# Query, index-query and z projections with 512 moving columns per matmul, in slabs of half the contraction

## What is computed

```
h = rmsnorm(x, attn_norm)
q, k, v, iq, ik, iw, z, xbc, dt, gate_a, gate_b = split(h @ w_in)     # widths 1024, 256, 256, 512, 64, 8, 2048, ...
q, k, iq, ik: head norms and partial rope
y_attn = sparse attention(q, k, v, iq, ik, iw)
y_ssd  = state-space scan(conv(xbc), dt)
y = y_ssd * silu(z)
y_ssd = y * rsqrt(mean(y^2) over each of 4 groups of 512) * ssd_norm
merged = sigmoid(gate_a) * (y_attn @ w_attn_branch) + sigmoid(gate_b) * (y_ssd @ w_ssd_branch)
```

## Time and profile before

| | |
|---|---|
| median of 3 runs | 1435.93 us (1435.58 to 1440.99) |
| the profiled execution | 1435.79 us |
| its span, first to last instruction | 1434.0 us |
| mean granted clock of TensorE | 0.969 |
| PE busy | 1341.9 us (94%) |
| PEld, DVE, ACT, POOL busy | 1223.3, 933.8, 755.3, 197.5 us |
| q to iq, on PE | 675.7 to 721.8 us |
| z, on PE | 971.5 to 1019.5 us |

### The profile page before, as it was taken

How to read it: one execution, slowest core, us unless ns; L and a number is a source line. 1 busy time by engine, 2 the same in 40 slices (tenths; PEclk the granted TensorE clock), 3 DMA queues, 4 the chain that set the end, 5 groups by cost and what they waited for, 6 DMA issues and landing times.

```text
span 1434.0 us, 22961 instructions
## 1 busy us (share of the span) xinstructions
PE 1341.9 (94%) x9038; PEld 1223.3 (85%) x9038; DVE 933.8 (65%) x1331; ACT 755.3 (53%) x1108; POOL 197.5 (14%) x163
## 2 busy tenths in 40 slices
PE   5999999979898999998989897989999999999998
PEld 5999989979698999988979787889999877787776
DVE  4655554474575555565379674584664799999996
ACT  4334345545634333355445676333653577778774
POOL 0211120021001111120020331230000000202020
PEclk9999999999999999999989899998999899999999
DMA  7666554533153665644634333324555399999991
GB/s 246 211 189 188 179 162 151 176 118 118 37 162 116 205 188 181 190 148 131 187 90 141 96 118 119 89 59 123 172 176 181 122 365 367 367 367 338 369 342 64
DMA packets 222165, 263.43 MB, mean 184 GB/s; under 512 B 14018, under 2 KB 204799, under 8 KB 221951
## 3 DMA queue, kind: packets, MB, share of 16 engines
q1 hardware_dynamic: 219520, 260.39, 56.8%
q10 hardware_dynamic: 2558, 1.86, 0.4%
HBM read 261.17 MB, written 1.05 MB: 183 GB/s over the span
## 4 chain that ended last, share of the span: by engine, by line
PE 75%; DVE 14%; ACT 6%; issue 2%; POOL 1%; DMA 1%; ACTq 0%; DVEq 0%; POOLq 0%
PE bank L526 23%; PE bank L528 22%; PE bank L527 22%; DVE sb_wlo L483 3%; DVE sb_wlo L470 3%; PE bank L621 1%; DVE sb_XC L1880 1%; PE bank L2502 1%; ACT sb_whi L464 1%; ACT sb_aw L1546 1%; DMA sb_pos<-in_positions 1%; DVE sb_st L1120 1%; PE bank L2565 1%; PE bank L2537 0%; ACT sb_sgh L1115 0%
## 5 line engine op out<-in xcount | busy, mean ns | idle before, releaser
L470 DVE TENSOR_TENSOR sb_wlo<-sb_raw,sb_whi 128x1024 fp32r<-128x1024 f32 (+4 forms) x306 | 389.4, 1316 | 224.3 <-ACT sb_whi L464 224.2
L464 ACT ACTIVATE sb_whi<-sb_raw 128x1024 fp32r<-128x1024 f32 (+4 forms) x306 | 301.4, 1037 | 238.4 <-PE bank L528 238.2
L526 PE MATMUL bank<-sb_Uh,sb_whi 128*128 128x256 f32 x1216 | 348.9, 287 | 9.2 <-DVE sb_wlo L470 5.2
L527 PE MATMUL bank<-sb_Ul,sb_whi 128*128 128x256 f32 x1216 | 346.6, 285 | 0.0
L528 PE MATMUL bank<-sb_Uh,sb_wlo 128*128 128x256 f32 x1216 | 346.4, 285 | 0.0
L526 PEld LDWEIGHTS bank<-sb_Uh,sb_whi 128*128 128x128 f32 x1216 | 236.0, 194 | 13.1 <-issue 10.1
L527 PEld LDWEIGHTS bank<-sb_Ul,sb_whi 128*128 128x128 f32 x1216 | 236.1, 194 | 0.8
L528 PEld LDWEIGHTS bank<-sb_Uh,sb_wlo 128*128 128x128 f32 x1216 | 235.9, 194 | 0.0
L526 PE MATMUL bank<-sb_whi,sb_Uh 128*128 128x256 f32 (+3 forms) x560 | 159.5, 285 | 1.1 <-DVE sb_Ul L611 0.7
L527 PE MATMUL bank<-sb_wlo,sb_Uh 128*128 128x256 f32 (+3 forms) x560 | 159.2, 284 | 0.0
L528 PE MATMUL bank<-sb_whi,sb_Ul 128*128 128x256 f32 (+3 forms) x560 | 159.1, 284 | 0.0
(11 more groups left out here) (408 smaller groups left out, 2250.3 us busy)
## 6 DMA issues: line engine op xcount, KB each, us to landing
sb_raw<-in_w_in SPq DMA_DIRECT2D x104, 512.0 KB, 4.4
sb_raw<-in_ffn_w_in SPq DMA_DIRECT2D x88, 512.0 KB, 4.5
sb_raw<-in_ffn_w_out SPq DMA_DIRECT2D x44, 512.0 KB, 3.7
sb_raw<-in_w_down SPq DMA_DIRECT2D x26, 512.0 KB, 6.9
sb_raw<-in_w_gate SPq DMA_DIRECT2D x25, 512.0 KB, 6.8
sb_raw<-in_w_up SPq DMA_DIRECT2D x25, 512.0 KB, 7.2
sb_raw<-in_w_out SPq DMA_DIRECT2D x16, 512.0 KB, 4.5
sb_raw<-in_w_ssd_branch SPq DMA_DIRECT2D x16, 512.0 KB, 4.4
```

Of the source, the lines that this page charges most:

```text
L464: nc.scalar.activation(whi[:, i % NSLOT, c], raw[:, i % NSLOT, c], ACT.Copy).then_inc(S("hi_done"), 1)
L470: nc.vector.tensor_tensor(wlo[:, i % NSLOT, c], raw[:, i % NSLOT, c], whi[:, i % NSLOT, c].bitcast(F32), ALU.subtract).then_inc(S("lo_done ...
L526: pe.matmul(o, lh, rh, start=start, stop=False, skip_group_check=True)
L527: pe.matmul(o, lh, rl, start=False, stop=False, skip_group_check=True)
```

## The change

q, iq and z are no longer cut into slabs of 8 chunks x 256 columns but into pairs of slabs of 4 chunks x 512 columns: the first slab of a pair holds chunks 0 to 3, the second chunks 4 to 7 of the same columns. A new function takes a pair through PE. It claims two banks, one for each token tile, and for each chunk moves 512 columns for tile 0 and 512 for tile 1, so that both banks are complete only after the second slab. It waits for each half of a slab by itself. The copies out, the silu and the multiplication take a bank as one token tile by 512 columns; both banks of a pair wait for its second slab. k, v, ik_dt and all other slabs stay.

```
+        def slab_pair(names, src):
+            for half, nm in enumerate(names):
+                slab(nm, src[:, KD // 2 * half:KD // 2 * (half + 1)], KD // 2, 512)
...
+        def tiles_by_halves(names, banks, xh, xl):
+            for half, nm in enumerate(names):
+                i = slab_of[nm]
+                wh, wl = wslab(i, KD // 2, 512)
+                stage = fresh.pop() if fresh else None
+                for k in range(KD):
+                    if not half * KD // 2 <= k < (half + 1) * KD // 2:
+                        continue
+                    r = k - half * KD // 2
+                    if r % 2 == 0:
+                        pe.wait_ge(*reach("lo_done", 2 * i + r // 2 + 1))
+                    if stage is not None:
+                        pe.wait_ge(*reach(stage[0], k + 1))
+                    for t in range(NT):
+                        tk = slice(t * P, (t + 1) * P)
+                        last = mm3(bank[banks[t]][:, :], xh[:, k, tk], xl[:, k, tk], wh[:, r], wl[:, r], k == 0, k == KD - 1)
...
+                last.then_inc(S("slab_used"), 1)
...
-                used(act, nm)
-                act.activation(dst, tok(b, n, HD + IH if n == SH else 0), ACT.Copy).then_inc(S("b2_ev"), 1)
+                used(act, {"q0": "q1", "q2": "q3", "iq0": "iq1"}[nm] if nm in ("q0", "q2", "iq0") else nm)
+                act.activation(dst, bank[b][:, :] if n == 512 else tok(b, n, HD + IH if n == SH else 0), ACT.Copy).then_inc(S("b2_ev"), 1)
...
             for c in range(8):
                 hi_upto(f"z{c}")
-                used(act, f"z{c}")
+                used(act, f"z{c | 1}")
...
-                v = XS[:, :, c * 256:(c + 1) * 256]
-                dve.tensor_tensor(v, v, sgh[:, c % 2].rearrange("p (t n) -> p t n", t=NT), ALU.mult).then_inc(S("yz"), 1)
+                v = XS[:, c % 2, c // 2 * 512:(c // 2 + 1) * 512]
+                dve.tensor_tensor(v, v, sgh[:, c % 2], ALU.mult).then_inc(S("yz"), 1)
...
-            for c in range(8):
-                s_ = need(f"z{c}")
-                claim(c % 4, "z_s", c + 1)
-                by_token(s_, c % 4, Uh, Ul, KD, 256).then_inc(S("slab_used"), 1)
+            for c in range(0, 8, 2):
+                for t in range(NT):
+                    claim((c + t) % 4, "z_s", c + t + 1)
+                tiles_by_halves((f"z{c}", f"z{c + 1}"), (c % 4, c % 4 + 1), Uh, Ul)
```

More of the change, by code:

```diff
@@ L347, in two_blocks @@
         w2 = view("w_in_2")
-        for i in range(4):
-            slab(f"q{i}", w2[:, :, i * 256:(i + 1) * 256], KD, 256)
-        for nm, lo, hi in (("k", C2_K, C2_V), ("v", C2_V, C2_IQ), ("iq0", C2_IQ, C2_IQ + 256), ("iq1", C2_IQ + 256, C2_IK)):
+        def slab_pair(names, src):
+            for half, nm in enumerate(names):
+                slab(nm, src[:, KD // 2 * half:KD // 2 * (half + 1)], KD // 2, 512)
+        for i in range(2):
+            slab_pair((f"q{2 * i}", f"q{2 * i + 1}"), w2[:, :, i * 512:(i + 1) * 512])
+        for nm, lo, hi in (("k", C2_K, C2_V), ("v", C2_V, C2_IQ)):
             slab(nm, w2[:, :, lo:hi], KD, hi - lo)
+        slab_pair(("iq0", "iq1"), w2[:, :, C2_IQ:C2_IK])
         slab("ik_dt", (w2[:, :, C2_IK:C2_Z], w2[:, :, C2_DT:C2_GA]), KD, C2_Z - C2_IK + SH)
@@ L368, in two_blocks @@
         gate_slab2(5)
-        for i in range(8):
-            slab(f"z{i}", w2[:, :, C2_Z + i * 256:C2_Z + (i + 1) * 256], KD, 256)
+        for i in range(4):
+            slab_pair((f"z{2 * i}", f"z{2 * i + 1}"), w2[:, :, C2_Z + i * 512:C2_Z + (i + 1) * 512])
         gate_slab2(6)
@@ L569, in by_token @@
             return last
+        def tiles_by_halves(names, banks, xh, xl):
[14 more added lines that the diff above has]
+                        last = mm3(bank[banks[t]][:, :], xh[:, k, tk], xl[:, k, tk], wh[:, r], wl[:, r], k == 0, k == KD - 1)
+                if stage is not None:
+                    fresh.append(stage)
+                last.then_inc(S("slab_used"), 1)
+            if fresh:
+                fresh.pop()
         def need(name):
@@ L1474, in _ @@
             tok = lambda b, n, at=0: bank[b].rearrange("p (t n) -> p t n", t=NT)[:, :, at:at + n]
-            outs = [(f"q{i}", i, xn[:, :, i * 256:(i + 1) * 256], 256) for i in range(4)]
+            outs = [(f"q{i}", i, xn[:, i % 2, i // 2 * 512:(i // 2 + 1) * 512], 512) for i in range(4)]
             outs += [("k", 4, K2[:].rearrange("p t h d -> p t (h d)"), 256), ("v", 5, V2[:], 256),
-                     ("iq0", 6, IQ[:, :, 0:4].rearrange("p t h d -> p t (h d)"), 256),
-                     ("iq1", 7, IQ[:, :, 4:8].rearrange("p t h d -> p t (h d)"), 256),
+                     ("iq0", 6, IQ[:, 0].rearrange("p h d -> p (h d)"), 512), ("iq1", 7, IQ[:, 1].rearrange("p h d -> p (h d)"), 512),
                      ("ik_dt", 0, IKW[:], HD + IH), ("ik_dt", 0, ssm[:, 0:2], SH)]
@@ L2350, in _ @@
                                          ("ik_dt", 0))):
-                s_ = need(nm)
                 claim(b, "b2_ev", n + 1 if n < 8 else 10)
-                by_token(s_, b, Uh, Ul, KD, slabs[s_][2]).then_inc(S("slab_used"), 1)
+                if nm in ("q0", "q2", "iq0"):
+                    claim(b + 1, "b2_ev", n + 2)
+                    tiles_by_halves((nm, nm[:-1] + str(int(nm[-1]) + 1)), (b, b + 1), Uh, Ul)
+                elif nm not in ("q1", "q3", "iq1"):
+                    s_ = need(nm)
+                    by_token(s_, b, Uh, Ul, KD, slabs[s_][2]).then_inc(S("slab_used"), 1)
             def xbc(j):
```

## The result

The changed kernel takes 1451.34 us (median of 4 runs, 1448.23 to 1453.12) against 1438.00 us of the kernel before beside it (1435.58 to 1440.99): ratio 1.0099, interval 1.0084 to 1.0114. By the medians that is 13.3 us, by the ratio 14.2. The profiled execution has 1453.12 us, the longest of the four.

The account below looks back on a forecast made before the run. TensorE, busy 94% of the span, was taken as the bound, with waits on ACT and DVE chains at stage ends. The sum was 1435.79 - 4.5 + 0.3 + 1.9 = 1433.5 us, range 1430.5 to 1439.

Parts of the forecast that it names:

- part 3: Pair banks read only behind the second slab: free inside stages if the odd slab's split is in time; waits at ends.
- something unseen: The chance of 0.03 left for an outcome that no listed case described.
- Part 1: In q, iq and z, 336 pairs of narrow matmuls become wide ones, 0.0134 us saved each: -4.5 us.
- the rival that rested on such a pace: Wide matmuls in q, iq and z start 0.131 us apart, saving 36.6 us: 1401.4 us; chance 0.02.
- Part 2: Slabs and transfers: same count, bytes and splits, memory rows of 2 KB instead of 1 KB; costed at nothing.
- After iq1: DVE's split of xbc1 ends later than the first head sum began before, delaying that chain: +0.3 us.
- After z7: DVE's chain of multiplication, splits and scaling makes YTl, and so the start of ws, later: +1.9 us.
- The rival of the clock: The clock falls in the longer wait before ws, costing 1.8 to 3.6 us: 1435.3 to 1437.1; chance 0.25.
- The rival of the odd slab: Splits of q3, z3, z5 and z7 come late, PE losing 2.6 us at four places: 1443.9 us; chance 0.05.

Follow-up runs that it names:

- e1: The changed kernel without the second claims of banks 1, 3 and 7 at q1, q3 and iq1: 1433.87 us, ratio 0.9981 to the kernel before.
- e3: The changed kernel with only q and iq in pairs, without second claims, z as before the change: ratio 0.9984 to the kernel before.
- e5: The kernel of e1 with DVE's split of ws01 moved behind YTl: 1431.13 us, ratio 0.9959 to the kernel before.
- e2: The changed kernel with only z in pairs, q and iq put back as before: ratio 0.9998 to the kernel before.
- e4: The changed kernel, second claims kept, with 14 zero-tile matmuls ahead of each: 1442.76 us, ratio 1.0045 to the kernel before.
- e6: The changed kernel with only the second claim of bank 7, ahead of ik_dt, taken out: ratio 1.0052 to the kernel before.
- e7: The changed kernel, second claims kept, with ACT copying both banks of a pair before splitting the next slab: ratio 1.0028 to the kernel before.

## Where the prediction was right and where it was wrong

**The step that failed** is in part 3. From "both banks of a pair are read only behind its second slab" it concludes: "Inside the stages this costs nothing as long as the split of the odd slab comes in time". That is a term put at nothing. I asked of PE behind a pair only which slab it needs, and not which banks it claims. The bank half of that question was answered for z, where the loop runs over pairs, and taken over for q and iq, where the loop runs over slabs and claims for each. Its price was 3 x 3.22 us of standing and some 8 to 9 us of half clock. The time left the range (1430.5 to 1439.0) by 12 us. Nothing in the forecast's list of rivals had this mechanism; only the 0.03 for something unseen covered it.

**Part 1, the wide matmuls: right.** In the z stage of the changed kernel, from 1000 to 1034 us, the three lines of a group of three start 0.23, 0.23 and 0.22 us apart; in iq, 47 intervals take 732.85 - 722.17 = 10.68, 0.2272 each. Forecast 0.2270, from the FFN's rows; the experts' 0.2330 was the wrong neighbour. z took 45.72 us (989.29 to 1035.01) instead of 48.03: 2.3 saved, 2.6 forecast. The Trainium skill (TensorE: Matmul & The Clock Gate, "Back-to-back issue gap") has 131 ns for N = 512; the rival that rested on such a pace had a chance of 0.02. No row here shows it: the trace has 227 ns, and the measurement decides.

**Part 2, transfers: right.** No PE wait for a slab appears in the pairs. The median from issue to landing of the w_in loads is 4.3 us on the page, beside 4.4.

**After iq1: right.** Without the second claims the chain can be read. In e1 the first head sum starts directly behind DVE's splits, as forecast:

```profile
723.54 4.74 DVE L477 TENSOR_TENSOR sb_wlo<-sb_raw,sb_whi 128x1024 fp32r<-128x1024 f32 x4 [10.32 <-ACT sb_whi L471]
728.20 0.21 DVE L1150 TENSOR_REDUCE sb_st<-sb_sgh 128x1 f32<-128x64 f32 x1
```

From q0 to it e1 needs 50.71 us, 1.62 less than before, where PE had gained 1.87 up to ik_dt. So 0.25 us are lost behind iq1, and as much in e3 and e5; +0.3 was forecast. In the changed kernel itself ACT comes later than DVE (6.59 us of idle time before the head sum), and the term does not show.

**After z7: right in its mechanism.** 14.76 for YTl, as worked out; ws 0.4 later than forecast, by the clock. e5 shows that the chain is the cause.

**The rival of the clock** happened, and it should have had more than 0.25: in all six profiles with the wait of 2.45 us ahead of the second transposes (the changed kernel, e1, e2, e4, e6, e7) the clock falls behind it, and in none of the three with 0.58 (before, e3, e5). Its price was about half of the 1.8 us given. In the changed kernel the clock is at 0.50 while the last transposes run, and is back 1.1 us after ws begins. From the first YTl to the start of ws it takes 4.11 us instead of 3.70, and to the start of the 30th matmul of ws 8.10 (1049.97 to 1058.07) instead of 7.17 (1032.62 to 1039.79): 0.9 us lost, 0.6 to 1.1 in the six.

```profile
1052.00:1054.70 2.70, 2.70 (x15) 2.48 (x14) 2.70 (x9) 2.33 (x7) 0.00 (x0) 0.50 0.57 180
```

So 1.9 + 0.9 us are lost behind z7, where the wide matmuls save 2.3 in z; half a microsecond is less than e2's interval can tell from nothing. The row that the prediction gives for a clock that is down after a pause of 4 us (733 to 737) has a mean of 0.98, since the fall lies at its very end; in the trace before, the clock is at 0.50 from 737 to 747.

The fallen clock is also what doubled the bill between q and ik_dt. I had priced it for one place and one wait; it goes with every wait of 3 us that the change adds.

**The rival of the odd slab** did not happen: none of q3, z3, z5 and z7 is waited for. It stood for "slower", and the slower result came by another way, from a wait for ACT's copies.

## What to carry to other kernels

When a loop over items becomes a loop over pairs, look at what it still does for the second item: a claim, a wait or an increment left there is a synchronisation with one's own work. Compare the waits of every instruction that follows the changed part, at each place where the same helper is used, and not at one of them. And add the clock to a new wait of TensorE where the rows show that it falls behind such a wait: here 3.2 us of standing cost 1.6 to 3.7 us more.

## What the runs showed of the hardware

Behind each of the three waits of 3.2 us in the changed kernel, and behind both in e6, the granted clock fell to 0.50. In three of the five it fell during the wait, in the other two 1.5 and 1.1 us after PE had gone on. Behind the waits of 1.3 us in e7 it fell once in three times, 2.5 us after the wait had ended. Behind the wait of 2.45 us ahead of the second transposes it fell in six profiles of six, behind that of 0.58 us in none of three. Matmuls on a zero tile in the wait kept the clock at 1.00 (e4).

A matmul with 104 moving columns starts 0.110 us after the last one (ik_dt in e1: 5.18 us for 47 intervals), one with 256 after 0.120, one with 512 after 0.227. So the step from 104 to 256 columns costs 0.010 us, and the step from 256 to 512 costs 0.107. Going from 256 to 512 columns therefore halves the number of matmuls and takes only (0.2404 - 0.2270) / 0.2404 = 5.6% off their time. Widening pays from narrow matmuls up to 256 columns, where 152 more columns cost 0.010 us, and hardly above.
